# The routing tables of an expert layer: later places and combined weights moved from VectorE to GpSimd, the exponential ahead of the gathered rows, the list product two quarters sooner

## The reference, cut to what matters

```python
def moe_swiglu(h, router, w_gate, w_up, w_down):
    t = h.reshape(b * s, d)
    logits = (t @ router).astype(jnp.float32)
    top_logits, top_idx = lax.top_k(logits, TOP_K)
    top_w = jax.nn.softmax(top_logits, axis=-1)
    combine = jnp.einsum('tk,tke->te', top_w, jax.nn.one_hot(top_idx, N_EXPERTS))
    out = jnp.zeros_like(t)
    for e in range(N_EXPERTS):
        out = out + combine[:, e:e + 1] * swiglu(t, w_gate[e], w_up[e], w_down[e])
```

## Time and profile before

| | |
|---|---|
| median of 3 runs | 1545.7 us (1545.66 to 1546.49) |
| profiled execution | 1543.8 us, its span 1541.9 us |
| TensorE busy | 1517.4 us, 98% |
| VectorE busy | 1316.3 us, 85% |
| ScalarE busy | 1108.6 us, 72% |
| GpSimd busy | 67.6 us, 4% |
| mean HBM rate | 295 GB/s over the span |

### The profile page before, as it was taken

The page is one execution under the profiler, slowest core; times in us unless marked ns, Lnnn a source line. Parts: engine busy times, 40 slices in busy tenths (PEclk is TensorE's granted clock), DMA queues, the critical chain, the costliest instruction groups (busy, mean ns, idle before and its releaser), DMA issues.

```text
span 1541.9 us, 23666 instructions
## 1 busy us (share of the span) xinstructions
PE 1517.4 (98%) x8529; PEld 1307.7 (85%) x8529; DVE 1316.3 (85%) x1557; ACT 1108.6 (72%) x1331; POOL 67.6 (4%) x66
## 2 busy tenths in 40 slices
PE   8999999999999999999999999999999999999997
PEld 7879899999999897888888888888888888888886
DVE  6776777777898779999999999999999999999996
ACT  6776444445678757878888788788788778878785
POOL 2001100010010000000000000000000000000000
PEclk9999999999999999999999999999999999999999
DMA  9335445455343389999999999999999999999980
GB/s 346 120 131 198 169 166 208 173 204 175 132 161 137 123 308 397 377 394 383 384 391 361 383 393 353 387 393 352 393 387 350 394 387 351 393 386 352 394 325 12
DMA packets 189044, 455.72 MB, mean 296 GB/s; under 512 B 4321, under 2 KB 5573, under 8 KB 188976
## 3 DMA queue, kind: packets, MB, share of 16 engines
q1 hardware_dynamic: 185472, 444.31, 77.8%
q0 software_dynamic: 3360, 10.44, 2.6%
q10 hardware_dynamic: 144, 0.07, 0.0%
HBM read 449.53 MB, written 5.26 MB: 295 GB/s over the span
## 4 chain that ended last, share of the span: by engine, by line
issue 57%; PE 33%; DVE 4%; ACT 3%; POOL 1%; DMA 1%; POOLq 0%; SPq 0%; DVEq 0%; ACTq 0%
PE bank L709 32%; ACT split_mem L1244 1%; POOL mem L687 1%; DVE split_mem L1708 1%; DMA h_rows<-mem 1%; POOL out L679 1%; ACT mem L1367 0%; DVE mem L1896 0%; DVE mem L1921 0%; ACT L1203 0%; DVE split_mem L2287 0%; DMA mem<-x 0%; ACT mem L1368 0%; ACT mem L1380 0%; DVE mem L1736 0%
## 5 line engine op out<-in xcount | busy, mean ns | idle before, releaser
L709 PE MATMUL bank<-split_mem 128*128 128x512 f32 (+1 forms) x7680 | 1440.4, 347 | 5.0 <-ACT mem L1368 1.4
L709 PEld LDWEIGHTS bank<-split_mem 128*128 128x128 f32 x7680 | 1224.4, 189 | 187.5 <-issue 6.7
L2287 DVE TENSOR_TENSOR split_mem<-mem,split_mem 128x1024 fp32r<-128x1024 f32 x668 | 806.6, 1223 | 66.1 <-ACT split_mem L1590 24.4
L1590 ACT CAST split_mem<-mem 128x1024 fp32r<-128x1024 f32 x672 | 705.0, 1051 | 190.4 <-PE bank L709 189.4
L1708 DVE TENSOR_TENSOR split_mem<-mem,split_mem 128x1024 fp32r<-128x1024 f32 x172 | 214.8, 1256 | 87.2 <-ACT split_mem L1244 86.3
L1244 ACT CAST split_mem<-mem 128x1024 fp32r<-128x1024 f32 x172 | 178.0, 1044 | 136.9 <-PE bank L709 135.6
L1597 ACT ACTIVATE mem<-bank,small 96x512 f32<-96x512 f32 x56 | 38.4, 686 | 2.1 <-DVE small L2232 2.1
L709 PE MATMUL bank<-mem 128*64 128x256 f32 (+8 forms) x290 | 35.3, 337 | 3.2 <-DVE mem L1921 1.7
L2294 DVE TENSOR_TENSOR mem<-mem,bank 96x512 f32<-96x512 f32 x56 | 37.9, 676 | 0.0
L1896 DVE SCALAR_TENSOR_TENSOR mem<-mem,colA 128x253 f32<-128x253 f32 (+2 forms) x72 | 32.1, 486 | 3.8 <-ACT mem L1333 2.3
L1149 PEld LDWEIGHTS bank<-cst,mem 96*128 96x128 f32 x224 | 24.4, 140 | 11.9 <-DVE mem L2294 4.9
(11 more groups left out here) (222 smaller groups left out, 486.0 us busy)
## 6 DMA issues: line engine op xcount, KB each, us to landing
mem<-moe_w_gate SPq DMA_DIRECT2D x56, 2048.0 KB, 9.7
mem<-moe_w_up SPq DMA_DIRECT2D x56, 2048.0 KB, 9.8
mem<-moe_w_down SPq DMA_DIRECT2D x56, 2048.0 KB, 10.1
mem<-ssd_w_in SPq DMA_DIRECT2D x10, 2048.0 KB, 8.0
mem<-ffn_w_gate SPq DMA_DIRECT2D x7, 2048.0 KB, 7.9
mem<-ffn_w_up SPq DMA_DIRECT2D x7, 2048.0 KB, 8.3
mem<-ffn_w_down SPq DMA_DIRECT2D x7, 2048.0 KB, 7.9
mem<-attn_w_in SPq DMA_DIRECT2D x4, 2048.0 KB, 13.9
```

Source lines behind the costliest of these rows:

```text
L709: return nc.tensor.matmul(o, lhsT, rhs, start=start, stop=stop, skip_group_check=shared)
L1590: nc.scalar.copy(wsplit[:, EXPERT_BUFFER[n % SPLITS], 0, :].rearrange("p (k n) -> p k n", n=w.shape[2]), quarter(w, q)).then_inc(w_hi, 1)
L2287: tt_(lo, quarter(w, q), hi.bitcast(F32), ALU.subtract).then_inc(w_lo, 1)
```

## The change

- GpSimd multiplies the difference by the rate, then makes the later places, and, when the shares are there, both weights, the combined weights and the columns of cj, each chained result with a link of its own (pool_step). It signals table_ready. The one fused operation of a later place becomes two.
- VectorE keeps of it the sum of one and the exponential and its reciprocal, between its gathered_first and the last split of ("gate", 0), and signals share_ready. It waits for table_ready before the places of the next job. The memset of this_weight stands alone in front of the third quarter.
- ScalarE takes the exponential before gathered_first, and loads the SiLU table behind it.
- TensorE makes the list product before the second quarter of ("up", 0), not before the fourth.

```diff
@@ -517,7 +517,7 @@
         hid_hi = sem("hid_hi")
         hid_ready = sem("hid_ready")
         y_ready_e = sem("y_ready_e")
-        table_ready = sem("table_ready")
+        table_ready, share_ready, pool_step = sem("table_ready"), sem("share_ready"), sem("pool_step")
 
 
         def cols(w, c0):
@@ -666,6 +666,33 @@
             pool.dma_start(out[0].rearrange("(a p) n -> p a n", p=P), xnat[:, :, :]).then_inc(summed, 16)
             pool.wait_ge(token_rate, 1)
             pool.dma_start(gain_row, norm_ffn[1:2, :].broadcast_to([P, D])).then_inc(in_gain_row, 16)
+
+            pool_link = Chain(pool, pool_step).link
+            G_ = nc.gpsimd
+            oh1, oh2, comb = (oh[:, j, :].rearrange("p (t e) -> p t e", e=E) for j in (0, 1, 3))
+            tmp, under = (tw[:, j, :].rearrange("p (t e) -> p t e", e=E) for j in (2, 7))
+            difference, ratio, w1, w2 = (tw[:, j, 0:TT] for j in (0, 1, 8, 9))
+            rate, place = cj[:, :, JOBS + 1], rj[:, :, 0:E]
+            pool.wait_ge(place_ready, 1)
+            G_.tensor_tensor(difference, difference, rate, ALU.mult).then_inc(top_diff, 1)
+            for p in range(1, PASSES):
+                later = rj[:, :, p * E:(p + 1) * E]
+                pool_link(G_.tensor_scalar(under, place, float(p * SLOTS), float(T), ALU.is_lt, ALU.mult))
+                pool_link(G_.tensor_scalar(later, place, -float(p * SLOTS), None, ALU.add))
+                pool_link(G_.tensor_tensor(later, later, under, ALU.add))
+            G_.memset(rj[:, :, JOBS:JOBS + 1], -1.0)
+            pool.wait_ge(share_ready, 1)
+            pool_link(G_.tensor_tensor(w1, w1, rate, ALU.mult))
+            pool_link(G_.tensor_tensor(w2, w1, ratio, ALU.mult))
+            G_.tensor_tensor(comb, oh1, w1.unsqueeze(2).broadcast_to([P, TT, E]), ALU.mult)
+            pool_link(G_.tensor_tensor(tmp, oh2, w2.unsqueeze(2).broadcast_to([P, TT, E]), ALU.mult))
+            pool_link(G_.tensor_tensor(comb, comb, tmp, ALU.add))
+            G_.tensor_copy(cj[:, :, 1:1 + E], comb)
+            for p in range(1, PASSES):
+                pool_link(G_.tensor_scalar(under, place, float(p * SLOTS), None, ALU.is_ge))
+                pool_link(G_.tensor_tensor(cj[:, :, 1 + p * E:1 + (p + 1) * E], comb, under, ALU.mult))
+            G_.tensor_copy(cj[:, :, 0:1], C("token").unsqueeze(2)).then_inc(table_ready, 1)
+
             pool.wait_ge(rows_ready, 4)
             pool.dma_start(h_rows.rearrange("(a p) n -> p a n", p=P), xnat[:, :, :]).then_inc(in_h_rows, 16)
             pool.wait_ge(in_h_rows, 16)
@@ -1155,9 +1182,8 @@
                         pe.wait_ge(free[1 + q], job * USES[1 + q] + BASE[1 + q])
 
                 def list_inside(q):
-                    if q == 0:
+                    if q == 1:
                         B.released(pe, "rank")
-                    if q == 3:
                         first_list()
 
                 for c in range(NC_F):
@@ -1557,7 +1583,6 @@
 
                 act.wait_ge(top_diff, 1)
                 fn(tw[:, 1, 0:TT], tw[:, 0, 0:TT], ACT.Exp).then_inc(top_exp, 1)
-                nc.scalar.preload_act_table(ACT.Silu)
 
             def gathered(job):
                 for half in range(2):
@@ -1612,8 +1637,9 @@
                     if tile == ("gate", 0):
                         if first:
                             router_turns()
+                            second_weight()
                             gathered_first()
-                            second_weight()
+                            nc.scalar.preload_act_table(ACT.Silu)
                             nc.scalar.copy(small[:, 32:33], small[:, 24:25]).then_inc(y_ready_e, 2)
                         else:
                             copy_result(job)
@@ -2176,43 +2202,6 @@
                 B.released(dve, "rank")
                 V_.tensor_copy(flag[:, 1:2], flag[:, 0:1]).then_inc(flag_ready, 1)
 
-            rate = cj[:, :, JOBS + 1]
-            under = per_expert(tw[:, 7, :])
-            w1, w2, den = tw[:, 8, 0:TT], tw[:, 9, 0:TT], tw[:, 10, 0:TT]
-
-            def rated_difference():
-
-                dve.wait_ge(token_rate, 1)
-                tt_(tw[:, 0, 0:TT], tw[:, 0, 0:TT], rate, ALU.mult).then_inc(top_diff, 1)
-
-            def later_places():
-
-                for p in range(1, PASSES):
-                    later = rj[:, :, p * E:(p + 1) * E]
-                    link(ts_(under, place, float(p * SLOTS), float(T), ALU.is_lt, ALU.mult))
-                    link(stt(out=later, in0=place, scalar=-float(p * SLOTS), in1=under, op0=ALU.add, op1=ALU.add))
-                V_.memset(rj[:, :, JOBS:JOBS + 1], -1.0)
-
-            def two_weights():
-
-                dve.wait_ge(top_exp, 1)
-                link(ts_(den, tw[:, 1, 0:TT], 1.0, None, ALU.add))
-                link(V_.reciprocal(w1, den))
-                link(tt_(w1, w1, rate, ALU.mult))
-                link(tt_(w2, w1, tw[:, 1, 0:TT], ALU.mult))
-
-            def combined_weights():
-
-                tt_(comb, oh1, w1.unsqueeze(2).broadcast_to([P, TT, E]), ALU.mult)
-                link(tt_(tmp, oh2, w2.unsqueeze(2).broadcast_to([P, TT, E]), ALU.mult))
-                link(tt_(comb, comb, tmp, ALU.add))
-                V_.tensor_copy(cj[:, :, 1:1 + E], comb)
-                for p in range(1, PASSES):
-                    link(ts_(under, place, float(p * SLOTS), None, ALU.is_ge))
-                    link(tt_(cj[:, :, 1 + p * E:1 + (p + 1) * E], comb, under, ALU.mult))
-                V_.memset(this_weight, 0.0).then_inc(this_ready, 1)
-                V_.tensor_copy(cj[:, :, 0:1], C("token").unsqueeze(2)).then_inc(table_ready, 1)
-
             def gathered_first():
 
                 for half in range(2):
@@ -2274,10 +2263,8 @@
                     for q in range(4):
                         if tile == ET[0] and q == 1:
                             gathered(job)
-                        if first and tile == ("up", 0) and q == 1:
-                            two_weights()
                         if first and tile == ("up", 0) and q == 2:
-                            combined_weights()
+                            V_.memset(this_weight, 0.0).then_inc(this_ready, 1)
                         if tile == ET[-1] and q == 2:
                             hidden_lo(NC_F - 1)
                         n = 4 * EXPERT[tile] + q
@@ -2322,6 +2309,7 @@
                         hidden_lo(c - 1)
                     if tile == ("up", 1):
                         take_list(job)
+                        dve.wait_ge(table_ready, 1)
                         places(job + 1)
                     if tile == ("up", 3):
                         next_list(job)
@@ -2334,10 +2322,11 @@
             pass_places()
             first_lo(1)
             first_lo(2)
-            rated_difference()
             gathered_first()
+            dve.wait_ge(top_exp, 1)
+            link(ts_(tw[:, 10, 0:TT], tw[:, 1, 0:TT], 1.0, None, ALU.add))
+            V_.reciprocal(tw[:, 8, 0:TT], tw[:, 10, 0:TT]).then_inc(share_ready, 1)
             first_lo(3)
-            later_places()
             job_body(0, True)
             with dve.Fori(1, E) as job:
                 job_body(job)
```

## The result

The changed kernel takes 1546.56 us (median of 22 runs, 1545.43 to 1549.96), the kernel before 1544.02 us in the same sessions (22 runs, 1542.54 to 1546.89). The ratio is 1.0017, 95% interval 1.0011 to 1.0022: slower by 2.5 us, within the 0.2% that the prediction set as its bound for "no change". The forecast was +2.2 us. The spans of the two profiled executions, 1541.9 and 1544.1 us, differ by 2.2.

A forecast was written before the change was run, and what follows sets the result against it. TensorE bounds the expert layers; "gate" 1 would start at 595.8 in place of 593.57, because the start is later and TensorE waits for the table. So 1545.7 + 2.2 = 1547.9 us, range 1544.0 to 1551.2.

The forecast's parts named there:

- The bound, and that a stall of the first job is kept: Expert layers: TensorE is the bound, busy 98%, so a first-job stall, added or removed, carries to the kernel's end.
- The start 1.1 us later: First expert job: GpSimd's product waits for VectorE's splits, so gathered rows come 1.1 us later and TensorE starts at 581.4.
- The price of a link: GpSimd's chain: 0.2 us per tiny instruction plus 0.1 hand-over, 0.3 a link.
- How many pass before the last split ends: GpSimd's eleven instructions: four pass in gaps between VectorE's splits, seven remain at 589.2, taking 2.1 us.
- The standstill: TensorE, before the second quarter of "up" 0, waits 3.0 us for the table, from 588.3.
- rival C: After TensorE's standstill the clock falls to 1.2 GHz, three quarters take 4.1 us more, 1552.0; chance 0.05.
- the forecast's case: Four or so GpSimd instructions pass through the split gaps; +0.8 to +3.0 us, 1546.5 to 1548.7; chance 0.5.
- Rival A: GpSimd's chain is hidden, two instructions at each split or none held; 1543.7, or 1544.8 with late start; chance 0.2.
- Rival B: Longer GpSimd links, 0.44 each, or no gaps used, give +3.1 us or more; chance 0.25.

The follow-up runs named there:

- e1: Changed kernel with six unread 256-column matmuls on TensorE before its wait for the table; 1544.94 us, ratio 1.0007 to the kernel before.
- e4: Changed kernel with VectorE waiting for the table before its split of the second quarter of "up" 0; 1543.04 us, ratio 0.9994 to the kernel before.
- e6: Changed kernel with the list product before the fourth quarter and VectorE's list copies behind its first split of "gate" 1; 1544.32 us, ratio 0.9997.
- e3: Kernel before with only the list product moved before the second quarter of "up" 0, tables still on VectorE; 1544.57 us, ratio 0.9997.
- e7: e6 with three unread 256-column matmuls in TensorE's router-stage wait; 1543.36 us, ratio 0.9992 to the kernel before.
- e10: Changed kernel with only three unread matmuls added in TensorE's router-stage wait; 1546.42 us, ratio 1.0014 to the kernel before.
- e5: Changed kernel with only rated difference and later places on GpSimd; both weights, combined weights on VectorE, list before fourth quarter; 1544.17 us, ratio 0.9999.

## Why the prediction was right, and where it wasn't

The forecast was +2.2 us and the measured difference +2.5, inside the 0.2% taken as no change. The time forecast, 1547.9, was set on the median of three runs, 1545.7; with 22 runs the kernel before takes 1544.02, so the 1546.56 lies 1.3 under the forecast, in its range. The mechanism was the predicted one: splits on VectorE hold the GpSimd instructions, one to a split, the list comes a microsecond sooner than before in place of two quarters, and TensorE stands still before a quarter that could have run. But **the sum was right partly because two errors offset each other**.

- *The bound, and that a stall of the first job is kept*: right. 2.72 us in the stretch of one execution, 2.5 in the medians.
- *The start 1.1 us later*: this step failed. The product passed at the border of two overlapping splits (end 577.71), the exponential ran at 577.74, and the gathered rows started at 578.17, TensorE at 580.40. The prediction had read from one instruction that GpSimd gets no turn between two overlapping VectorE instructions. In the trace after it does so repeatedly: 583.63 plus 1.20 ends inside the pair of splits from 583.55 to 585.91. The lower bound given for the start, no delay, was the true value.
- *The price of a link*: 0.3 taken; the last six, from 588.60 to 590.23, took 0.27 each, with 0.19 to 0.26 for the instruction.
- *How many pass before the last split ends*: four taken, five measured, since the one that is held by the last split ends with it. Seven of 0.3 left at 589.2 against six of 0.27 left at 588.5, so the list at 591.35 against 590.32. One microsecond of that is the start that wasn't late.
- *The standstill*: 3.0 forecast, 2.86 measured. Without a fallen clock the change would have cost 1.10 us (e1).
- *The clock*: rival C, at a chance of 0.05. It came, on top of the forecast's case, and its price was 1.62 us, not 4.1: the half clock lasted only from about 590.7 to 594.2, far shorter than three quarters at that clock, and the list's 0.3 fell outside it. The mistake was to treat it as unlikely because the longest wait until then, 1.7, had not shown it; a standstill of 2.9 was outside what that row could speak for. And that the clock never left its upper level was true of the one profiled execution only: 35 of 87 others had a low mean clock. The Trainium skill (TensorE: Matmul & The Clock Gate, HAM oscillation) gave the warning, and here the trace bears it out: 2.86 us without a matmul, then the lower level.
- *Rival A* fell: at each of the five splits one instruction passed, not two. *Rival B* (a longer link) did not occur: the links were shorter than its 0.44.

So the account is: 1.10 us for the late table and 1.62 for the clock. The prediction had 2.2 for the former, of which 1.1 was a start that didn't come late, and nothing for the latter. That the total came out near 2.5 is luck to that extent.

The Trainium skill's rule, cited in the prediction, that a VectorE instruction with two SBUF inputs and a GpSimd one that reads SBUF exclude each other (SBUF — State Buffer, Who interferes with whom) is borne out here by e4 (1.28 against 0.22 for one instruction) and e6 (1.29 against 0.26).

## What to carry to other kernels

A tiny instruction on GpSimd is cheap, 0.2 us, only while VectorE isn't working on two SBUF operands; beside a stream of such instructions each link of a chain took one of them (five links, five splits), so count links, not work. Place the consumer of such a chain where the waiting engine still has other work: the same moved tables cost 2.7 us with the list product early and saved 1.0 with it late. And price a new standstill of TensorE with its clock: a wait longer than any that the trace has shown is not covered by the clock that the trace shows.

## What was not expected of the hardware

- After a standstill of 2.86 us TensorE's granted clock fell to 1.2 GHz for about 3.4 us; after 1.33 us (e3) and 1.12 us (e6, e7) it did not. It fell only when TensorE had gone on: 0.4 us after the start of the list in the changed kernel, about 1.4 us after it in e10 (list at 591.27, clock 0.65 in 592.50 to 593.00). The length of the wait alone doesn't decide it: in the router stage it fell in e4's and e5's profiles and not in the kernel before's, behind the same wait of 0.95 us.
- In 35 of 87 executions of the kernel before, the mean clock was low and the time 2.3 us longer on average. In e5's profile the fall was seen in the router stage, behind small matmuls and a wait of 0.95 us. With three matmuls in that wait the low mean came in none of 33 executions. That e1, which changes nothing there, also has none in eleven is not explained; the rounded mean, which includes the kernel's start, is a coarse sign.
- GpSimd gets in between two overlapping VectorE instructions when it has waited for a whole one, and doesn't slow them: the pair of splits from 583.55 took 2.36 us with one of its instructions passing between them, as a pair without one did. The pair from 585.87 took 2.58, but there the second split had to wait for ScalarE's cast, which ended at 587.20. Whether an instruction that arrives shortly before the border misses it, as the one at 454.94 did, was not tried.
